# Prompt attention of a hybrid decoder step: score and value products as three 16-bit products each

## What is computed

```
def dsa_attend(q, qi, wi, q_pos, k, v, ki, k_pos, topk):
    ...
    _, idx = lax.top_k(score, topk)
    ...
    s = jnp.einsum('btkgd,btskd->btkgs', qg, k_sel) * (HEAD_DIM ** -0.5)
    dist = (q_pos[None, :, None] - sel_pos).astype(f32)
    s = s - slopes[None, None, :, :, None] * dist[:, :, None, None, :]
    s = jnp.where(valid[:, :, None, None, :], s, -jnp.inf)
    p = jax.nn.softmax(s, axis=-1)
    o = jnp.einsum('btkgs,btskd->btkgd', p, v_sel)
```

## Time and profile before

| what | value |
|---|---|
| runs, us | 1857.0, 1854.83, 1860.35; median 1857.0 |
| span of the profiled execution | 1859.2 us; no time outside the span is listed for it, and it lies 2.2 us above the median and among the runs |
| busy over the span | PE 1779.6, PEld 1210.3, DVE 1017.3, ACT 832.5, POOL 302.8 us |
| block_d ("attend") | 1244.0 to 1420 us of the span |
| PE line 1757 (scores) | 73.6 us busy |
| PE line 1743 (values) | 72.9 us busy |
| PE line 1733 (transposes) | 40.4 us busy |

### The profile page before, as it was taken

The page is one execution under the profiler, slowest core; times in us unless marked ns, Lnnn a source line. Parts: engine busy times, 40 slices in busy tenths (PEclk is TensorE's granted clock), DMA queues, the critical chain, the costliest instruction groups (busy, mean ns, idle before and its releaser), DMA issues. The chain is left out here.

```text
span 1859.2 us, 30880 instructions
## 1 busy us (share of the span) xinstructions
PE 1779.6 (96%) x12569; PEld 1210.3 (65%) x12569; DVE 1017.3 (55%) x1951; ACT 832.5 (45%) x1399; POOL 302.8 (16%) x217
## 2 busy tenths in 40 slices
PE   6999999999999999999999996998999899999997
PEld 4565555556666666666666664774554488888886
DVE  6564136547978687686868440554543752221226
ACT  5554557664344344333434321654443863333331
POOL 3022210111111121121212111026202300000000
PEclk9999999999999999999999998999999899999999
DMA  9522121112222322322232207503223722222224
GB/s 359 156 91 69 56 64 47 58 47 81 77 70 81 81 77 81 81 77 69 81 82 77 85 24 283 192 7 79 59 74 106 274 70 70 93 71 69 75 88 188
DMA packets 192289, 179.83 MB, mean 97 GB/s; under 512 B 30674, under 2 KB 171634, under 8 KB 189522
## 3 DMA queue, kind: packets, MB, share of 16 engines
q1 hardware_dynamic: 171938, 137.15, 24.0%
q10 hardware_dynamic: 14640, 22.96, 3.4%
q0 software_dynamic: 5568, 17.72, 2.8%
HBM read 143.59 MB, written 34.20 MB: 96 GB/s over the span
## 5 line engine op out<-in xcount | busy, mean ns | idle before, releaser
L703 PE MATMUL ps<-h,w 128*128 128x352 f16 (+2 forms) x6096 | 943.7, 315 | 1.6 <-PEq L223 1.0
L703 PEld LDWEIGHTS ps<-h,w 128*128 128x128 f16 (+1 forms) x6096 | 595.2, 99 | 333.4 <-issue 16.8
L987 POOL TENSOR_TENSOR w<-wb,w 128x2048 f16<-128x2048 f32 x44 | 184.0, 4182 | 812.1 <-ACT w L834 812.1
L2463 PE MATMUL ps<-w_f,m 128*128 128x256 f16 x2688 | 295.8, 273 | 4.4 <-DVE y_room L2538 2.9
L2463 PEld LDWEIGHTS ps<-w_f,m 128*128 128x128 f16 x2688 | 262.3, 98 | 36.6 <-issue 6.4
L1204 DVE MAX8 m<-score 128x8 f32<-128x1024 f32 (+2 forms) x192 | 171.6, 893 | 5.7
L1205 DVE MATCH_REPLACE8 score<-m,score 128x1024 f32<-128x1024 f32 (+2 forms) x192 | 168.1, 875 | 0.0
L842 ACT ACTIVATE zst<-ps,unit 128x352 f32<-128x352 f32 (+1 forms) x88 | 49.8, 582 | 252.1 <-PE ps L703 228.6
L2553 DVE SCALAR_TENSOR_TENSOR y_room<-ps,unit_f,x_f 128x256 f32<-128x256 f32 (+1 forms) x64 | 30.8, 483 | 219.5 <-PE ps L2463 189.6
L1196 DVE SCALAR_TENSOR_TENSOR score<-room,wis,score 128x1024 f32<-128x1024 f32 (+5 forms) x90 | 92.7, 1030 | 78.5 <-ACT room L904 73.0
L830 ACT ACTIVATE wb<-wb,unit 128x2048 f32<-128x2048 f32 x44 | 88.1, 2003 | 89.9 <-DVE unit L1004 89.9
(11 more groups left out here) (477 smaller groups left out, 1818.1 us busy)
## 6 DMA issues: line engine op xcount, KB each, us to landing
wb<-in_w_in_dram SPq DMA_DIRECT2D x44, 1024.0 KB, 5.0
z_scratch<-zst ACTq DMA_DIRECT2D x32, 528.0 KB, 2.7
score<-in_w_out_dram SPq DMA_DIRECT2D x7, 2048.0 KB, 11.6
y_room<-z_scratch SPq DMA_DIRECT2D x8, 1056.0 KB, 18.0
x_in<-in_x_prompt_dram SPq DMA_DIRECT2D x8, 1024.0 KB, 8.8
w_kv<-in_w_mem_kv_dram POOLq DMA_DIRECT2D x16, 512.0 KB, 6.9
x_f<-in_x_prompt_dram SPq DMA_DIRECT2D x8, 1024.0 KB, 5.2
out_y_p_dram<-y_room SPq DMA_DIRECT2D x7, 1024.0 KB, 3.9
```

Of the source, the lines that this page charges most:

```text
L703: last = nc.tensor.matmul(ps[0:m, n, 0:w], w16[:, b, pw_, k, 0:m], h16[:, ph, k, t0:t0 + w], start=(k == 0 and i == 0), stop=(k == KT - 1 ...
L987: nc.gpsimd.tensor_tensor(w16[:, b, 1, :, 0:w], wb[:, b, :, 0:w], w16[:, b, 0, :, 0:w], ALU.subtract).then_inc(w_split, 1)
L2463: last = nc.tensor.matmul(ps[:, bank(b, i), 0:SLAB], m16[:, mp, k, t * P:(t + 1) * P], weights(s, b, wp, k), start=(k == 0 and j == 0), st ...
```

## The change

In `block_d` the queries, keys, values and turned probabilities are each split into a 16-bit high and low half, and scores and value products become three 16-bit matmuls into the same PSUM place.

- Each key block's turned probabilities are now rounded by ScalarE (`high_turned`) and the rest by VectorE (`low_turned`), both for every block, in place of one copy by one of them. `low_turned` waits for `p_high`.
- Queries of tile t + 1 are split by ScalarE at (2t + 1, j = 2) and VectorE at (2t + 1, j = 3); those of tile 0 at the end of `block_c`. Keys are split in `block_c`, values at the start of `block_d`, in two pieces.
- The scales come from `fit`, made on VectorE at the start of `block_c` (`fit_halves`), from `head_unit`, which `set_unit` writes. `set_unit` has one operation more a chunk, and a root taken on the bits in place of a mean of absolute values (ScalarE: Square in place of Abs, the same instructions).
- GpSimd scales `kmq` and copies the high keys into place; its scaling of `kT` goes. The queries of tile 1 are loaded after that copy.
- The custom operation and the gate product take their factor from `fit`, not as an immediate.

```diff
@@ block_b, set_unit
-                link(TSC(u[0], u[0], W_SHIFT, TINY, ALU.mult, ALU.max))
+                link(TSC(u[0], u[0], LEAST, None, ALU.max))
+                bits = u[0].bitcast(I32)
+                link(TSC(bits, bits, 0.5, HALF_BIAS, ALU.mult, ALU.add))
                 nc.vector.reciprocal(u[1], u[0])
...
+def high_queries(nc, act, v, t):
+    act.wait_ge(v["q_loaded"][t % 2], 64 * (t // 2 + 1))
+    nc.scalar.activation(query_halves(v, t % 2)[0], queries(v["v_or_q"])[:, t % 2], ACT.Copy,
+                         scale=v["fit"][:, Q_FIT:Q_FIT + 1]).then_inc(v["q_high"], 1)
+
+def low_queries(nc, dve, v, t):
+    dve.wait_ge(v["q_high"], BATCHES + t + 1)
+    high, low = query_halves(v, t % 2)
+    nc.vector.scalar_tensor_tensor(out=low, in0=queries(v["v_or_q"])[:, t % 2], scalar=v["fit"][:, Q_FIT:Q_FIT + 1], in1=high,
+                                   op0=ALU.mult, op1=ALU.subtract).then_inc(v["q_low"], 1)
@@ block_c, scalar
             gate(2)
+            act.wait_ge(fitted, BATCHES + 1)
+            act.wait_ge(kv_turned, QT + 1)
+            nc.scalar.activation(k_room_high, kT[:, :, 0:SEQ], ACT.Copy, scale=fit[:, K_FIT:K_FIT + 1]).then_inc(k_split, 1)
             act.wait_ge(mk_turned, 1)
             nc.scalar.activation(mkT_flat, ps[:, 6:8, :].rearrange("p a n -> p (a n)"), ACT.Copy).then_inc(mk_copied, 1)
...
+            high_queries(nc, act, v, 0)
@@ block_c, vector
+            low_queries(nc, dve, v, 0)
@@ block_d, tensor
             def turn(u, k):
                 gk = first_key_block[u] + k
                 if gk >= 2:
-                    pe.wait_ge(p_copied[gk % 2], gk // 2)
+                    pe.wait_ge(p_low, gk - 1)
...
-                v_ = kv_tok[:, k, 256 + g * P:256 + (g + 1) * P]
-                nc.tensor.matmul(ps[:, 6 + u % 2, :], v_, prT[:, gk % 2, :, :].rearrange("p j n -> p (j n)"),
-                                 start=(k == 0), stop=(k == t)).then_inc(o_mm, 1)
+                for i, (a, b) in enumerate(((0, 0), (1, 0), (0, 1))):
+                    if i == 2:
+                        pe.wait_ge(p_low, gk + 1)
+                    last = nc.tensor.matmul(ps[:, 6 + u % 2, :], v_16[a][:, k, g * P:(g + 1) * P], prT[:, gk % 2, b, :],
+                                            start=(k == 0 and i == 0), stop=(k == t and i == 2))
+                last.then_inc(o_mm, 1)
...
-                            last = nc.tensor.matmul(ps[:, 2 * (hh % 2) + x0 // 512, 0:w], q_t[:, t % 2, GQA * g + j, :],
-                                                    kT[:, g, x0:x0 + w], start=True, stop=True)
+                            for i, (a, b) in enumerate(((0, 0), (0, 1), (1, 0))):
+                                last = nc.tensor.matmul(ps[:, 2 * (hh % 2) + x0 // 512, 0:w], q_16[a][:, GQA * g + j, :],
+                                                        k_16[b][:, g, x0:x0 + w], start=(i == 0), stop=(i == 2))
@@ block_d, scalar
+            def high_turned(todo):
+                for u, k in todo:
+                    gk = first_key_block[u] + k
+                    act.wait_ge(p_turned, gk + 1)
+                    if gk >= 2:
+                        act.wait_ge(o_mm, gk - 1)
+                    nc.scalar.activation(prT[:, gk % 2, 0, :], ps[:, 4 + gk % 2, :], ACT.Copy, scale=P_SHIFT).then_inc(p_high, 1)
+            for n, x in enumerate(V_PIECES):
+                if n:
+                    act.wait_ge(v_split, SPLITS_BEFORE + 2)
+                nc.scalar.activation(v_16[0][:, x, :], kv_tok[:, x, N_KV * P:], ACT.Copy, scale=fit[:, V_FIT:V_FIT + 1]).then_inc(v_split, 1)
             for s in range(len(UNITS) + 1):
                 for j in range(GQA):
+                    if j == 2 and s % 2 == 1 and (s + 1) // 2 < QT:
+                        high_queries(nc, act, v, (s + 1) // 2)
...
-                    copy_turned(act, nc.scalar.copy, turned_at(s, j), 0)
+                    high_turned(turned_at(s, j))
@@ block_d, vector
+            def low_turned(todo):
+                for u, k in todo:
+                    gk = first_key_block[u] + k
+                    dve.wait_ge(p_high, gk + 1)
+                    nc.vector.scalar_tensor_tensor(out=prT[:, gk % 2, 1, :], in0=ps[:, 4 + gk % 2, :], scalar=P_SHIFT, in1=prT[:, gk % 2, 0, :],
+                                                   op0=ALU.mult, op1=ALU.subtract).then_inc(p_low, 1)
...
+                    if j == 3 and s % 2 == 1 and (s + 1) // 2 < QT:
+                        low_queries(nc, dve, v, (s + 1) // 2)
...
-                    copy_turned(dve, nc.vector.tensor_copy, turned_at(s, j), 1)
+                    low_turned(turned_at(s, j))
```

More of the change, by code:

```diff
@@ L46 @@
 TINY = 1e-30
+ROOT_SHIFT = 2.0 ** -15
+LEAST = 1e-32
+HALF_BIAS = float(0x1FBD1DF5)
 SPAN = 8
@@ L142, in build_program @@
         ki_s = sb_in(top, "ki_s", [P, 2, NS])
+        head_unit = sb_in(top, "head_unit", [P, N_HEADS + 2 * N_KV])
+        fit = sb_in(top, "fit", [P, 10 + N_HEADS])
         mid = ExitStack()
@@ L1316, in _, with key_halves, query_halves @@
                         copy(st_out[:, 2 + n, :], ps[:, 5, n * P:(n + 1) * P]).then_inc(last_copied, 1)
+Q_FIT, K_FIT, V_FIT, AWAY_FIT, FAR_FIT, BACK_FIT, VALUE_FIT, HEAD_FIT = 3, 4, 5, 6, 7, 8, 9, 10
+SPLITS_BEFORE = BATCHES + 2
+P_SHIFT = 2.0 ** 14
+def key_halves(kT):
+    both = kT[:].bitcast(F16)
+    return both[:, :, SEQ:2 * SEQ], both[:, :, 0:SEQ]
+def query_halves(v, b):
+    low = queries(v["v_or_q"])[:, b, :, :].rearrange("p h n -> p (h n)").bitcast(F16)[:, 0:N_HEADS * P]
+    at = KT * TOK + (2 - 2 * b) * N_HEADS * P // 2
+    high = v["y_room"][:, at:at + N_HEADS * P // 2].bitcast(F16)
+    return high.rearrange("p (h n) -> p h n", h=N_HEADS), low.rearrange("p (h n) -> p h n", h=N_HEADS)
+def high_queries(nc, act, v, t):
[7 more added lines that the diff above has]
+                                   op0=ALU.mult, op1=ALU.subtract).then_inc(v["q_low"], 1)
 def block_c(nc, io, v, sem, sb_in):
@@ L1328, in block_c @@
         vT = v["v_or_q"][:].rearrange("p (g n) -> p g n", g=N_KV)
-        q_t, kmq, q_loaded = v["v_or_q"], v["kmq"], v["q_loaded"]
+        q_t, kmq, q_loaded, fit, head_unit = (v[n] for n in ("v_or_q", "kmq", "q_loaded", "fit", "head_unit"))
+        k_high, k_low = key_halves(kT)
+        k_room_high = q_t[:, SEQ:2 * SEQ].bitcast(F16).rearrange("p (g n) -> p g n", g=N_KV)
+        fitted, k_split, k_moved = (v[n] for n in ("fitted", "k_split", "k_moved"))
         qmT = sb("qmT", [P, 4, TOK])
@@ L1391, in _ @@
             sp.wait_ge(kv_copied, QT + 1)
-            for t in range(2):
-                load_queries(sp, queries(q_t), z_dram, t, q_loaded)
+            load_queries(sp, queries(q_t), z_dram, 0, q_loaded)
             for n, name in enumerate(("out_k", "out_v")):
@@ L1400, in _ @@
                 sp.dma_start(dst, kv_tok[0:NS, QT, part]).then_inc(kv_stored, 16)
+            sp.wait_ge(k_moved, BATCHES + 1)
+            load_queries(sp, queries(q_t), z_dram, 1, q_loaded)
             sp.wait_ge(kv_stored, 32 + 64)
@@ L1410, in _ @@
                                          pattern=[[-1, SEQ]], channel_multiplier=1))
-            pool.wait_ge(kv_turned, QT + 1)
-            for g in range(N_KV):
-                link(nc.gpsimd.tensor_scalar(kT[:, g, 0:SEQ], kT[:, g, 0:SEQ], SCALE, None, ALU.mult))
+            pool.wait_ge(fitted, BATCHES + 1)
+            link(nc.gpsimd.tensor_scalar(kmq[:], kmq[:], fit[:, AWAY_FIT:AWAY_FIT + 1], -1e38, ALU.mult, ALU.max))
+            pool.wait_ge(k_split, BATCHES + 2)
+            nc.gpsimd.tensor_copy(k_high, k_room_high).then_inc(k_moved, 1)
         @block.tensor
@@ L1531, in _, with fit_halves @@
             TSC, TT = nc.vector.tensor_scalar, nc.vector.tensor_tensor
+            def fit_halves():
+                reduce = nc.vector.tensor_reduce
+                reduce(fit[:, 0:1], head_unit[:, 0:N_HEADS], AX_X, ALU.max)
+                link(reduce(fit[:, 1:3], head_unit[:, N_HEADS:].rearrange("p (a g) -> p a g", a=2), AX_X, ALU.max))
+                link(TSC(fit[:, 0:3], fit[:, 0:3], 1.0 / Z_SHIFT, 1e-16, ALU.mult, ALU.max))
+                TSC(fit[:, VALUE_FIT:VALUE_FIT + 1], fit[:, 2:3], 1.0 / P_SHIFT, None, ALU.mult)
+                link(nc.vector.reciprocal(fit[:, Q_FIT:V_FIT + 1], fit[:, 0:3]))
+                link(TSC(fit[:, AWAY_FIT:AWAY_FIT + 1], fit[:, Q_FIT:Q_FIT + 1], fit[:, K_FIT:K_FIT + 1], 1.0 / SCALE, ALU.mult, ALU.mult))
+                TSC(fit[:, FAR_FIT:FAR_FIT + 1], fit[:, AWAY_FIT:AWAY_FIT + 1], FAR, -1e38, ALU.mult, ALU.max)
+                link(nc.vector.reciprocal(fit[:, BACK_FIT:BACK_FIT + 1], fit[:, AWAY_FIT:AWAY_FIT + 1]))
+                for h in range(N_HEADS):
+                    last = TSC(fit[:, HEAD_FIT + h:HEAD_FIT + h + 1], fit[:, BACK_FIT:BACK_FIT + 1], -SLOPES[h], None, ALU.mult)
+                last.then_inc(fitted, 1)
             def multiply(i):
@@ L1600, in block_d @@
         pr = sb("pr", [P, 2, GQA, SEQ])
-        prT = sb("prT", [P, 2, GQA, P])
```

(5 more changed lines are left out.)

64 lines of the change are left out of this document (42 added, 22 removed).

## The result

| | before | after |
|---|---|---|
| median of the runs, us | 1858.49 (four runs, 1854.83 to 1860.35) | 1895.61 (1902.78, 1896.92, 1894.29, 1889.65) |
| ratio after to before | | 1.0197, 95% interval 1.0178 to 1.0216 |
| span of the profiled execution | 1859.2 | 1901.1 (the execution of 1902.78) |
| PE busy | 1779.6 | 1769.4 |

The forecast was 1897 us, range 1880 to 1918; the time lies inside. TensorE is busy for less time, and the program takes longer. The profiled execution is the longest of the four, so the spans differ by more (41.9 us) than the medians (37.1 us).

A forecast was written before the change was run, and what follows sets the result against it. TensorE bounded block_b and block_d before; after the change a ring of VectorE and ScalarE sets block_d's pace. Terms 20.2 + 1.5 + 1.3 + 5.8 + 4.8 + 4.9 + 2 = 40.5 us on the 1857.0 median gave 1897 us, range 1880 to 1918.

The forecast's parts named there:

- ring, with its last step: block_d: custom operation, exponential, high half, low half, next custom operation set the pace; 193.3 us against 173.1, +20.2.
- clock: block_d, tiles 0 to 3: granted clock falls while TensorE is under 65% busy; +2 us, bounds 0 and 10.
- factor: block_d: factor read from `fit` costs 0.06 us in 64 custom operations and 16 gates; +4.8 us, bounds 0 and 5.
- queries: block_d: ScalarE wants the next tile's queries earlier and waits, low queries held once by GpSimd; +4.9 us, bounds 2 and 8.
- values at the block's start: Start of block_d: splitting values takes 4.15 us, waits for GpSimd 1.65; +5.8 us, bounds 4.2 and 8.
- block_c: Before the first logits, high keys delay a copy TensorE awaits, +1.5 us; low queries at the end, +1.3.
- set_unit: block_b: one added 0.15 us operation in 44 chunks stays covered, 0 us; 9 us if uncovered.
- signs: What would show it right, including TensorE's idle released by `prT` of VectorE and first custom operation 7 us after block_d's start.
- price of a low half: VectorE's subtraction in the ring of block_d: 0.62 us a block, taken from block_a.
- The high half as a copy: ScalarE's rounding in the ring of block_d: 0.57 us, 0.65 with two hand-overs.
- The clock rival: block_d, tiles 4 to 7: clock falls there too, costing 52 us if all is slow; half gives 1923 us; chance 0.13.
- The faster rival: block_d: TensorE keeps the pace because the low half does not wait behind the exponential; 1835 us; chance 0.06.

The follow-up runs named there:

- e3: Changed kernel with constant factors in the custom operation and gate in place of values from `fit`: 1888.6 us, 1.0160 of the kernel before.
- e6: Changed kernel with SyncE issuing the next tile's queries earlier, ahead of the reciprocals: 1888.7 us, 1.0159 of the kernel before.
- e4: Changed kernel with one more small VectorE operation in set_unit: 1891.2 us, 1.0175 of the kernel before.
- e1: Changed kernel with ScalarE's high halves moved ahead of the exponential, no operation added or removed: 1845.9 us, 0.9935 of the kernel before.
- e2: Changed kernel with a fourth score product (low half by low half) on TensorE: 1901.7 us, 1.0224 of the kernel before.
- e9: e7 with ScalarE's copy of a turned block moved ahead of the exponential: 1856.8 us, 0.9983 of the kernel before.
- e7: Changed kernel with only scores as three 16-bit products, values and turned probabilities 32-bit as before: 1861.2 us, 1.0008 of the kernel before.
- e10: e1 with earlier queries, values split by GpSimd in block_c, q_index copies and GpSimd's set-up moved later: 1834.4 us, 0.9852 of the kernel before.

## Why the prediction was right, step by step

| term | forecast | measured | from |
|---|---|---|---|
| ring, with its last step | +20.2 | +20.7 with the clock | 28.0 less the two lines below |
| clock | +2 | in the line above | |
| factor | +4.8 | +3.8 | e3 |
| queries | +4.9 | +3.5 | e6 |
| values at the block's start | +5.8 | +4.2 | marks |
| block_c | +2.8 | +4.2 (+2.3 to +2.7 where the clock stayed 1.00) | marks |
| set_unit | 0 | 0 | e4 |
| sum | 40.5 | 36.4; medians 37.1 | |

- **The number is better than the sum.** The forecast put 40.5 us on a median of 1857.0; the medians differ by 37.1, and the kernel before came out at 1858.5 with a fourth run. That 1897 is within 1.4 us of 1895.6 is in part luck; the ring with the clock, the values, the queries and the factor were each put too high by 1.0 to 1.6 us, block_c by 1.4 too low.
- **The ring** was the step on which all rested, and it is shown twice: by the trace (4.28 us a head against 4.26 worked out, 4.31 with the factor) and by e1, which takes 45 us away by order alone. That its price was not TensorE's is shown by e2. Two of the signs came otherwise than written: TensorE's value products were mostly released by `prT` of ScalarE (37.7 of 43.7 us), not of VectorE, since the first of the three products waits for the high half alone; and the first custom operation came 5.6 us behind the block's start, not 7.
- **The price of a low half** was taken from block_a, 0.62 us; two take 1.21 us to the next operation's start. The high half as a copy, 0.57: 0.61 from high half to low half.
- **Values: mis-sized.** I added 1.65 us for waits on GpSimd. There was none, and the lower bound of 4.2 was the answer. The last section has the rows.
- **Queries: mechanism right, size too large.** Tile 2's were issued 18.6 us after the block's start (I had 20) and ScalarE lost 2.2 us (2.6). For tile 3 ScalarE's rounding shows no wait. The low queries that GpSimd was to hold up took 1.32 us in the mean and 1.47 at most, not 2.3.
- **Block_c: too small, by a term for the clock that I had put at nothing.** The high keys took 1.99 us and began at 1169.56, as forecast ahead of the copy that TensorE waits for, and the low queries 1.28 at the end. But TensorE now stood 2.43 us ahead of the first logits, where it had stood 1.11, and in the 3.5 us from their start the granted clock was 0.56 (1.00 before). In e3 TensorE stood as long, and the clock stayed at 1.00. The changed kernel and e3:

```profile
1172.52:1176.02 3.50, 3.50 (x9) 2.87 (x10) 1.49 (x1) 1.25 (x1) 1.87 (x1) 0.56 1.02 409
```
```profile
1168.38:1171.88 3.50, 3.50 (x14) 2.63 (x15) 2.85 (x3) 1.25 (x1) 1.87 (x1) 1.00 1.03 410
```

  It stayed at 1.00 in e3, e6 and e9, which have 98.7 to 99.1 us for this stretch, 2.3 to 2.7 more than before, close to the 2.8 of the forecast. In the eight other changed kernels it was 0.53 to 0.71 there, and they have 100.4 to 101.9 us. Why it falls in some executions and not in others no run shows.
- **Factor:** 0.05 us in each custom operation (1221 to 1271 ns), where I had 0.06.
- **The clock rival** fell: 1.00 in tiles 4 to 7, though TensorE was busy only 28.2 of 35 us in tile 7. What the Trainium skill (TensorE: Matmul & The Clock Gate, on psum-queue depth-cycling) reports of such short idles did not occur here. In tiles 0 to 3 the clock fell lower and for longer than I thought, but the ring had room there, as worked out: what the sum leaves for it is under 2 us (20.7 us for ring and clock together, 20.2 forecast for the ring alone). No run set it apart in block_d. Where the ring was cut it may cost more, beside the wait for the queries: those tiles give e7 and e9 no gain.
- **The faster rival** (1835) fell as forecast, though its number is nearly what e10 reaches. It lacked the order, and e10 has earlier queries and an earlier start beside it, so that the numbers agree is luck.

## What to carry to other kernels

When an operation is split over two engines, write down for each engine what stands ahead of its half, follow the waits round, and sum the durations; if the sum is above the busiest engine's work, the new work is not what costs, the order is. Put work whose input is old (here blocks turned from the unit before) ahead of work whose input is being made. When a stretch gets faster, look at the queues beside it for the next thing that was in time only because all else was late.
